# Moving two of a linear unit's value chunks behind its output products, in a two-layer hybrid decoder step

## The reference, cut to what matters

```python
def step(S, inp):
    qc, kc, vc, bc = inp
    qe = qc.astype(f) * jnp.exp(bc)
    ke = kc.astype(f) * jnp.exp(-bc)
    att = jnp.where(causal, jnp.einsum('bchk,bshk->bhcs', qe, ke), 0.0)
    o = jnp.einsum('bhcs,bshv->bchv', att, vc.astype(f)) + jnp.einsum('bchk,bhkv->bchv', qe, S)
    kd = kc.astype(f) * jnp.exp(b_last[:, None] - bc)
    S = jnp.exp(b_last)[..., None] * S + jnp.einsum('bshk,bshv->bhkv', kd, vc.astype(f))
    return S, o
```

```python
k_past = cache_k[li, page_table].reshape(Bd, P, DA_HEADS, 2 * DA_DH)
v_past = cache_v[li, page_table].reshape(Bd, P, DA_HEADS, DA_VD)
out = (jnp.einsum('bhqk,bkhd->bqhd', a[..., :P], v_past.astype(jnp.float32))
       + jnp.einsum('bhqk,bkhd->bqhd', a[..., P:], v_new.astype(jnp.float32)))
```

## Time and profile before

| what | value |
|---|---|
| median of 3 runs | 1508.99 us (1508.52 to 1518.43) |
| the profiled execution's own time | 1519.64 us |
| its span, first to last instruction | 1517.6 us |
| mean granted TensorE clock in it | 0.943 |
| TensorE busy | 1394.1 us, 92% |
| VectorE busy | 881.0 us, 58% |
| ScalarE busy | 514.1 us, 34% |
| GpSimd busy | 334.8 us, 22% |
| HBM traffic | 163 GB/s over the span |

### The profile page before, as it was taken

How to read it: one execution, slowest core, us unless ns; L and a number is a source line. 1 busy time by engine, 2 the same in 40 slices (tenths; PEclk the granted TensorE clock), 3 DMA queues, 4 the chain that set the end, 5 groups by cost and what they waited for, 6 DMA issues and landing times.

```text
span 1517.6 us, 26186 instructions
## 1 busy us (share of the span) xinstructions
PE 1394.1 (92%) x11360; PEld 1260.6 (83%) x11360; DVE 881.0 (58%) x1161; ACT 514.1 (34%) x841; POOL 334.8 (22%) x268
## 2 busy tenths in 40 slices
PE   5999967787687899999999999899989999999997
PEld 5999833345343598999999999899989999999997
DVE  4799888776776527435344443789455343352443
ACT  3422254433242434212222122477443121221233
POOL 1577677776755100000000000000000000000000
PEclk8999978897777899999999999999999999999999
DMA  8688689998878721322332231222322233223211
GB/s 297 238 304 279 240 315 393 366 373 314 337 304 301 284 92 57 112 84 84 100 97 84 84 108 61 94 73 85 96 72 86 84 96 100 84 84 111 84 57 57
DMA packets 126856, 249.32 MB, mean 164 GB/s; under 512 B 5251, under 2 KB 107415, under 8 KB 110096
## 3 DMA queue, kind: packets, MB, share of 16 engines
q0 software_dynamic: 18432, 134.23, 23.4%
q1 hardware_dynamic: 105180, 109.46, 22.4%
q10 hardware_dynamic: 3132, 3.98, 0.9%
HBM read 239.99 MB, written 7.73 MB: 163 GB/s over the span
## 4 chain that ended last, share of the span: by engine, by line
PE 56%; issue 26%; DVE 7%; POOL 4%; DMA 3%; ACT 2%; another core or an unknown queue 0%; POOLq 0%; ACTq 0%; SPq 0%; DVEq 0%
PE PS L1910 45%; DMA KV<-in_cache_v,CIDX 3%; POOL PROD L698 2%; PE PS L2117 2%; DVE SC L1372 2%; PE PS L2201 1%; POOL KV L770 1%; PE PS L2278 1%; DVE ST L1610 1%; DVE SC L1384 1%; PE PS L1894 1%; DVE PROD L1382 1%; DMA XIN<-in_x_prompt 1%; PE PS L2222 1%; PE PS L2016 1%
## 5 line engine op out<-in xcount | busy, mean ns | idle before, releaser
L1910 PE MATMUL PS<-H_hi,W_hi 128*128 128x260 f32 x1936 | 399.9, 287 | 11.5 <-DVE H_lo L1347 9.7
L1910 PE MATMUL PS<-H_hi,W_lo 128*128 128x260 f32 x1936 | 394.8, 284 | 0.0
L1910 PE MATMUL PS<-H_lo,W_hi 128*128 128x260 f32 x1936 | 394.5, 284 | 0.0
L1910 PEld LDWEIGHTS PS<-H_hi,W_hi 128*128 128x128 f32 x1936 | 303.3, 190 | 15.6 <-issue 14.8
L1910 PEld LDWEIGHTS PS<-H_hi,W_lo 128*128 128x128 f32 x1936 | 301.9, 190 | 0.0
L1910 PEld LDWEIGHTS PS<-H_lo,W_hi 128*128 128x128 f32 x1936 | 301.7, 190 | 0.0
L1305 DVE TENSOR_TENSOR W_lo<-RAW,W_hi 128x2048 fp32r<-128x2048 f32 x90 | 206.2, 2292 | 115.4 <-ACT W_hi L828 113.3
L828 ACT ACTIVATE W_hi<-RAW 128x2048 fp32r<-128x2048 f32 x89 | 169.9, 1909 | 269.9 <-PE PS L1910 265.5
L1910 PE MATMUL PS<-U_hi,W_lo 128*128 128x260 f32 x1024 | 206.4, 283 | 0.0
L1910 PE MATMUL PS<-U_lo,W_hi 128*128 128x260 f32 x1024 | 206.0, 283 | 0.0
L1910 PE MATMUL PS<-U_hi,W_hi 128*128 128x260 f32 x1024 | 206.0, 282 | 0.0
(11 more groups left out here) (314 smaller groups left out, 1496.3 us busy)
## 6 DMA issues: line engine op xcount, KB each, us to landing
RAW<-in_w_up SPq DMA_DIRECT2D x32, 1024.0 KB
RAW<-in_w_down SPq DMA_DIRECT2D x32, 1024.0 KB
RAW<-in_w_in_even SPq DMA_DIRECT2D x13, 1024.0 KB
RAW<-in_w_in_odd SPq DMA_DIRECT2D x8, 1024.0 KB
RAW<-in_w_out_even SPq DMA_DIRECT2D x4, 1024.0 KB
RAW<-in_w_out_odd SPq DMA_DIRECT2D x4, 1024.0 KB
x_saved<-X ACTq DMA_DIRECT2D x1, 2080.0 KB, 12.6
X<-x_saved SPq DMA_DIRECT2D x1, 2080.0 KB, 7.8
```

The lines of the kernel that those rows point to most:

```text
L1910: t = MM_(PS[:, 2 * bank + j, 0:HALF], w[:, ch.slot, k, cols], x[:, k, halves[j]], start=k == 0 and n == 0, stop=k == KT - 1 and n == 2)
```

## The change

In each linear unit the second and third value chunk (steps 4 and 6 above) are taken from their places and summed together behind the output products of step 7, so ahead of the next unit's `inner_products`. The first chunk stays. No instruction is added or removed, the order of loads and POOL's program stay as they are.

```diff
             slot(GLA_SLOT + 2 * u + 1)
-            v_chunks(33 + 3 * u, 1)
             state_values(u)
             pe.wait_ge(st_ready, 8 * u + 8)
             if u:
                 normalise(15 + u)
-            v_chunks(34 + 3 * u, 1)
             if u:
                 pe.wait_ge(nev_done, outputs_done(16 + u))
             for par in range(2):
@@
                 t.then_inc(go_done, 1)
+            v_chunks(33 + 3 * u, 2)
         slot(GLA_SLOT + 16)
```

## The result

The changed kernel took 1524.22 us in the median of four runs (1522.85 to 1527.99), the kernel before 1510.1 on the same chip: ratio 1.0071, 95% interval 1.0049 to 1.0092. (The ratios given here are those on record; they are not quotients of two medians, which would be 1.0093 in this case.) Forecast were 1503.8, at the outside 1512. A later comparison gave 1.0031 (1.0015 to 1.0047). So the change costs 0.3 to 0.7%, 5 to 11 us, where a gain of 5.2 was forecast. Even so the two intervals above, for the same two kernels, don't overlap: a difference of 0.004 between ratios of different occasions proves nothing. Two single executions, of 2660.55 us (kernel before) and 2679.53 us (shorter filler), are in no ratio.

The account below looks back on a forecast made before the run. TensorE's work bounds most of the kernel; in the linear units engines take turns in a ring, none filling the stretch. Terms -8.2 + 2 + 1 = -5.2 us from the median 1509.0 gave 1503.8, range 1497 to 1512.

Parts of the forecast that it names:

- I take +2: Linear units: allowance in us for TensorE's clock falling after the new wait, chosen between 0 and +12.6.
- -7.9 at full clock: Units 0 to 6: gains of 4.5, 1.9 and 1.5 us in units 2, 4 and 5, nothing in the others.
- The rival that followed from it: Linear units: outputs and both chunks run at half clock after the idle time, +12.6 us, total 1514; chance 0.13.
- Unit 2, -4.5: Outputs no longer stand behind a third chunk waiting 5.36 us for weights; next attention products 4.0 to 5.1 us sooner.
- Unit 4, -1.9: Outputs start sooner and run faster without the half-speed third chunk ahead; clamp and next state chain 1.9 us earlier.
- unit 5, -1.5: Outputs start 1.1 us sooner, and normalisation no longer queues behind the slow second chunk (0.3 to 0.5).
- Units 1, 3, 6, nothing: No gain or loss: moved chunks fill time TensorE waited anyway, 2.1 us at full clock.
- Taking it out leaves TensorE idle there; that gives nothing back: Second chunk beside the serial state steps: 3.03 us of steps cover it wholly, so removing it gains nothing.
- The transpose behind the chunks: Next unit's transpose, masked keys and updates queue behind two chunks: even within 0.3 us at full clock, 3.3 late at half.
- signs of being wrong: Forecast would be wrong if waits for landings grow, or L2201 waits for L1029 in most units.
- Ring and tail, -0.3 and +1: Unit 7: outputs gain 0.3 us; later buffer release delays chunk 60's load by 5.4 us, costing 0 to 2.7, taken +1.
- Behind the linear units ... the gain should reach the end whole: After the linear units TensorE streams without such waits, so the gain should carry through unchanged.

Follow-up runs that it names:

- shorter filler: Changed kernel plus zero-weight matmuls: two of 512 columns between state values and the state-step wait, one of 256 behind each normalisation; ratio 0.9946 to the kernel before.

## Why the prediction failed, by its own steps

**"I take +2" for the clock is the step that failed.** The bounds were 0 and +12.6, and I chose near the low one because the gap was "nearer to rows 12". But in rows 12 the second chunk ends into the stretch and the third lies in it: TensorE was busy 3.69 of 4.60 us, so 0.9 us idle. The new gap leaves it busy 2.25 of 4.90 in unit 2, idle 1.93 us ahead of the normalisation and 0.71 ahead of the outputs, 2.6 in all. That lies between the 0.9 of rows 12 and the 5.36 of the earlier trace rows, no row decided it, and what follows it is what followed in rows 4. Measured in the pair: the units are even where -7.9 at full clock was forecast for them, so the clock took 7.8 in place of 2. In the changed order itself it took more: 127.5 to 127.7 us without filler, 113.9 to 117.8 with it, 10 to 14. That -7.9 was the right sum at full clock is not shown: against the 120.6 to 128.4 of the order before, 117.8 is a gain of 2.8 to 10.6.

The Trainium skill, page "TensorE: Matmul & The Clock Gate", section "Why this matters for your kernels", had asked for no long idle gaps between bursts. Here the trace agrees in the outcome, 0.50 to 0.54 in the block behind the gap, though the idle time was in two short pieces (1.93 and 0.71 us in unit 2). The rival that followed from it got a chance of 0.13; its price of +12.6 was too high for the units of the pair (7.8), and its 1514 too low for the whole, since it left out everything behind unit 7.

**Unit 2, -4.5**: -4.7 in its own step, and the outputs began at the copy as worked out. The mechanism was right; against all six profiles of the order before the gain is 3.1 to 4.7. What it didn't include is that part comes back in the next unit, +1.6 to +3.2 even when unit 2 alone is changed.

**Unit 4, -1.9; unit 5, -1.5**: -0.2 and -1.1, both with outputs and chunks at half speed. In the other profiles of the order before unit 4 took 14.9 to 16.9 us, less than the 17.4 after it, so the gain forecast there did not come.

**Units 1, 3, 6, nothing**: +2.4, +2.8, +0.8. "There the two moved chunks fill time in which TensorE waited anyway" holds for 2.1 us of chunks. They took 3.64. The text named "more than 2 us" as the point of decision, and that is what happened.

**"Taking it out leaves TensorE idle there; that gives nothing back"** (the second chunk beside the state steps) is true of the time in that place, but it left the clock out: TensorE's clock over these gaps fell to 0.74 to 0.78, where the stretch with both chunks in the earlier trace rows had 1.00.

**The transpose behind the chunks (8.4 against 5.1, 3.3 us late per unit)** was the wrong mechanism for the price. With the transpose ahead of the chunks nothing was won, since the waiting only moved to the normalisation. Both of the prediction's own signs of being wrong came: L2201 waited for L1029 six times (4.0 us), and the waits for landings grew to 2.37 and 2.27 us.

**Ring and tail, -0.3 and +1**: the request came at 498.14, within "494 to 499". But the stretch to the projection grew by 4.6 us in this pair and 6.6 in the second. With the request as late and the clock kept it took 31.5 and 33.4, so a late request alone, the +1 of the term, shows no price; what the term lacked is the half clock.

**"Behind the linear units ... the gain should reach the end whole"**: +2.6 us behind L1910. Here TensorE waits 2.3 us for each of the last two landings and comes into the projection at half clock. Of the eighteen profiles, the nine whose projection begins at a clock of 1.00 have 999.3 to 1000.7 us behind L1910, the nine that begin at 0.50 to 0.66 have 1001.3 to 1003.2. This can happen with unit 7 as before, too: the kernel that left unit 7 alone had 1002.3 there, and a clock of 0.53 in the first 4 us.

By terms: the units missed by 5.8 (-5.9 forecast with the clock term, -0.1 measured), the way to the projection by 3.9 (+0.7, +4.6), what is behind by 2.6; less 1.8 from the earlier start this makes 10.5, which is the distance of +5.3 from -5.2.

What stays open: how much of the first pair's +10.7 us (by the ratio; the medians lie 14.1 apart) is more than the 5.3 of its profiles; why the seven units of one order differ by up to 7.8 us between profiles, and with it how much the units lose by the change; and why the kernels with filler in seven units, with the shortest units, have no better ratio. Their profiles have 1001.3 and 1001.7 behind L1910 and again a half-clock start of the projection (0.50 and 0.66 in the first 4 us), which accounts for about 1 us of it.

## What to carry to other kernels

Work that lies beside another engine's serial chain, and so seems free to move, may be what keeps TensorE's clock for the work behind it. Before moving it, add up what TensorE still does in the gap and all its waits in it, and cost what follows at both clocks. If the stretch reads 0.5, put zero-weight matmuls in the gap, as the cheapest test: when the time falls although work was added, the clock was the bound. Take several profiles of each kernel before splitting a few us between stages. And look at the last iteration apart, since there the slow block meets consumers that have no slack.

## What the runs showed of the hardware

On one chip, 46 more matmul records (967 against 921 in the stretch, the shorter filler) took the changed kernel from 1529.76 us to 1516.19. Two idle pieces, 1.93 and 0.71 us in unit 2, 1.77 and 1.47 in unit 1, were followed by 8 us at 0.50, in one unit after another, which I had expected only of a wait like the 5.36 us in the earlier trace rows. The same instructions of units 0 to 6 took 120.6 to 128.4 us in six profiles, at clocks of 0.78 to 0.73. And the same kernel's median was 1510.1, 1513.99, 1514.8, 1522.29 and 1523.9 us on five occasions, a spread of 13.8 us, larger than the 11 us that the strongest ratio (0.9926) stands for, so that only ratios on one chip could tell them.
